# A recurrence in chunks: half of its level products on the off-diagonal quadrants of TensorE, and both parts of the output summed in PSUM

## What is computed

```
def step(s, inp):
    r_t, w_t, k_t, v_t, a_t, b_t = inp
    sa = jnp.einsum('bhvk,bhk->bhv', s, a_t)
    s = s * w_t[:, :, None, :] + sa[..., :, None] * b_t[:, :, None, :] + v_t[..., :, None] * k_t[:, :, None, :]
    return s, jnp.einsum('bhvk,bhk->bhv', s, r_t)
```

## Time and profile before

| | us |
|---|---|
| median of 3 runs (lowest, highest) | 2602.45 (2600.98, 2603.02) |
| the profiled execution, its own time | 2604.29 |
| its span in the trace | 2602.5 |
| TensorE busy in the span | 2314.5 (89%) |
| VectorE busy | 1688.6 (65%) |
| ScalarE busy | 1025.3 (39%) |
| GpSimd busy | 661.3 (25%) |
| granted TensorE clock, mean over the span | 0.933 |

### The profile page before, as it was taken

The page is one execution under the profiler, slowest core; times in us unless marked ns, Lnnn a source line. Parts: engine busy times, 40 slices in busy tenths (PEclk is TensorE's granted clock), DMA queues, the critical chain, the costliest instruction groups (busy, mean ns, idle before and its releaser), DMA issues. The chain is left out here.

```text
span 2602.5 us, 50127 instructions
## 1 busy us (share of the span) xinstructions
PE 2314.5 (89%) x20892; PEld 1847.3 (71%) x20892; DVE 1688.6 (65%) x2155; ACT 1025.3 (39%) x1633; POOL 661.3 (25%) x659
## 2 busy tenths in 40 slices
PE   5998988899999669999777999999973999999993
PEld 2886755568877558888636899997652888888883
DVE  5990559551115445666576776774657999999994
ACT  3112541231014420001154545444132877777773
POOL 1331568123320023222006666650000100000000
PEclk8998999999999779999878999998986999999997
DMA  6232004421104445211053111104142999999994
GB/s 237 96 124 75 1 33 142 132 99 45 49 14 185 151 156 193 96 41 40 14 185 92 32 32 29 29 20 169 57 174 97 409 407 396 396 393 405 396 378 158
DMA packets 136485, 401.77 MB, mean 154 GB/s; under 512 B 56314, under 2 KB 67834, under 8 KB 108754
## 3 DMA queue, kind: packets, MB, share of 16 engines
q1 hardware_dynamic: 124180, 360.02, 37.3%
q0 software_dynamic: 4608, 16.78, 2.7%
q10 hardware_dynamic: 7488, 21.99, 2.2%
HBM read 341.05 MB, written 57.69 MB: 153 GB/s over the span
## 5 line engine op out<-in xcount | busy, mean ns | idle before, releaser
L3900 DVE TENSOR_TENSOR ex_wl<-ew_raw,ex_wh 128x2048 fp32r<-128x2048 f32 x192 | 435.6, 2290 | 41.7 <-ACT ex_wh L3862 38.2
L3862 ACT ACTIVATE ex_wh<-ew_raw 128x2048 fp32r<-128x2048 f32 x192 | 367.6, 1919 | 109.5 <-PE ex_U L3806 40.3
L118 PE MATMUL sp_acc<-b2h_hi,sp_wh 128*128 128x512 f32 (+1 forms) x528 | 194.7, 369 | 16.2 <-POOL sp_wl L1729 16.2
L118 PE MATMUL sp_acc<-b2h_lo,sp_wh 128*128 128x512 f32 (+1 forms) x528 | 194.4, 368 | 0.0
L118 PE MATMUL sp_acc<-b2h_hi,sp_wl 128*128 128x512 f32 (+1 forms) x528 | 194.2, 368 | 0.0
L3783 POOL DMA_INDIRECT x<-ex_o,ex_at x16 | 26.5, 1656 | 490.2 <-DVE ex_o L3923 490.2
L2621 PE MATMUL rc_chain<-rc_x,rc_near 64*64 64x64 f32 x3200 | 132.8, 222 | 5.3 <-DVE rc_near L2503 2.2
L1727 POOL CAST sp_wh<-sp_w 128x1024 fp32r<-128x1024 f32 x26 | 28.3, 1088 | 402.2 <-DMA sp_w<-in_w_conv 221.4
L2621 PEld LDWEIGHTS rc_chain<-rc_x,rc_near 64*64 64x64 f32 x3200 | 111.1, 135 | 19.2 <-issue 9.0
L118 PEld LDWEIGHTS sp_acc<-b2h_hi,sp_wh 128*128 128x128 f32 x528 | 100.1, 190 | 33.9 <-POOL sp_wl L1729 16.6
L118 PEld LDWEIGHTS sp_acc<-b2h_lo,sp_wh 128*128 128x128 f32 x528 | 100.2, 190 | 16.4
(11 more groups left out here) (520 smaller groups left out, 5887.6 us busy)
## 6 DMA issues: line engine op xcount, KB each, us to landing
ew_raw<-in_exp_gate SPq DMA_DIRECT2D x64, 1024.0 KB, 8.0
ew_raw<-in_exp_up SPq DMA_DIRECT2D x64, 1024.0 KB, 9.5
ew_raw<-in_exp_down SPq DMA_DIRECT2D x64, 1024.0 KB, 8.0
b2p_pT<-in_ada_w SPq DMA_DIRECT2D x32, 512.0 KB, 6.0
...
```

Source lines behind the costliest of these rows:

```text
L118: ins = nc.tensor.matmul(out, w[a][:, k, :], h[b][:, k, cols], start=(first and n == 0), stop=(last and n == 2))
L3862: nc.scalar.activation(wh[:, n % RING], raw[:, n % RING], ACT.Copy).then_inc(q["w_hi"], 1)
L3900: V.tensor_tensor(wl[:, n % RING], raw[:, n % RING], wh[:, n % RING].bitcast(f32), ALU.subtract).then_inc(q["w_lo"], 1)
```

## The change

`chained_x` and `advanced` send half of their eight products (heads 2 and 3 of the four tiles, j = 1) through the off-diagonal quadrants. For that x is kept with its two row halves swapped in those tiles after the first product and swapped back after the second. The transposes must then swap the halves too: one `turned` becomes three instructions, one 128x128 in place and two of 64x128 that write the other half. Both products now go to PSUM as two banks of 128 columns. `outputs_of_state` is gone on TensorE and VectorE; its products accumulate in the same PSUM region as those of `outputs`, in four groups of four 64x64 and four 128x64 products. The hand-written orders of four engines are new; of GpSimd's and ScalarE's the diff below leaves the lists out, and of the other two the removed lines.

```diff
@@ -2132,7 +2132,7 @@
-        joint = {n: ph.sem(n) for n in ("firsts_done", "xi_done", "g_crossed", "g_done", "u_done", "y_done", "y_crossed", "s_done", "rows_done", "v_done")}
+        joint = {n: ph.sem(n) for n in ("firsts_done", "xi_done", "g_crossed", "g_done", "u_done", "y_crossed", "s_done", "rows_done", "v_done")}
...
@@ -2157,9 +2157,9 @@
-        def chained(d, bank):
-            return X[d][:, bank, 0:HP * CK].rearrange("p (h t) -> p h t", t=CK)
+        def chained(d):
+            return X[d][:, :, 0:2 * CK].rearrange("p j (f t) -> p j f t", t=CK)
@@ -2293,7 +2293,7 @@
                         if c >= 2:
                             pool.wait_ge(s["low_done"], c - 1)
                         if c >= CTX_CK + 2:
-                            pool.wait_ge(joint["y_done"], c - 1 - CTX_CK)
+                            pool.wait_ge(joint["y_crossed"], c - 1 - CTX_CK)
                         G.tensor_tensor(b["ar"][:, c % 2, :, CK:], rows(RB, c, d), b["e_in"], ALU.mult).then_inc(s["r_scaled"], 1)
@@ -2323,26 +2323,26 @@
...
@@ -2380,14 +2380,14 @@
                 def filled(c, d):
                     if runs(c):
                         if c >= 2:
-                            act.wait_ge(q[d]["xt_next"], LEVELS * (c - 1))
+                            act.wait_ge(q[d]["xt_next"], 3 * LEVELS * (c - 1))
                             act.wait_ge(q[d]["t1_done"], LEVELS * (c - 1))
                         A.activation(t[d]["x"][:, c % 2], spread(T.ident2[:], 1, HP), ACT.Copy, scale=-1.0).then_inc(q[d]["filled"], 1)
                 def factored(c, d, l):
                     if runs(c):
                         act.wait_ge(q[d]["t1_done"], LEVELS * c + l + 1)
-                        A.activation(t[d]["t1"][:], chained(d, 0), ACT.Copy).then_inc(q[d]["t1_ready"], 1)
+                        A.activation(paired(t[d]["t1"][:]), chained(d), ACT.Copy).then_inc(q[d]["t1_ready"], 1)
                     if runs(c):
...
@@ -2506,7 +2506,7 @@
                     if runs(c):
                         b, s = t[d], q[d]
                         dve.wait_ge(s["xp_done"], (LEVELS - 1) * c + l + 1)
-                        V.copy_predicated(b["x"][:, c % 2], spread(T.level[d][l + 1][:].bitcast(u32), 1, HP), chained(d, 1)).then_inc(s["x_next"], 1)
+                        V.copy_predicated(paired(b["x"][:, c % 2]), over(T.level[d][l + 1][:].bitcast(u32)), chained(d)).then_inc(s["x_next"], 1)
                 def turned(c, d, l):
                     if runs(c):
@@ -2517,7 +2517,14 @@
                                 dve.wait_ge(joint["xi_done"], c)
                         else:
                             dve.wait_ge(s["x_next"], (LEVELS - 1) * c + l)
-                        V.transpose(b["xt"][:].rearrange("p h t -> p (h t)"), b["x"][:, c % 2].rearrange("p h t -> p (h t)")).then_inc(s["xt_next"], 1)
+                        def flat(m):
+                            return m.rearrange("p h t -> p (h t)")
+                        near_half, far_half = slice(0, 2), slice(2, 4)
+                        V.transpose(flat(b["xt"][:, near_half]), flat(b["x"][:, c % 2, near_half])).then_inc(s["xt_next"], 1)
+                        for p in range(2):
+                            src, to = slice(p * CK, (p + 1) * CK), slice((1 - p) * CK, (2 - p) * CK)
+                            V.transpose(flat(b["xt"][to, far_half]), flat(b["x"][src, c % 2, far_half])).then_inc(s["xt_next"], 1)
                 def last_factor(c, d):
                     if runs(c):
@@ -2525,7 +2532,7 @@
                         dve.wait_ge(s["t1_done"], LEVELS * c + LEVELS)
                         if c:
                             dve.wait_ge(joint["xi_done"], c)
-                        V.copy_predicated(b["last_t"][:], spread(T.level[d][LEVELS][:].bitcast(u32), 1, HP), chained(d, 0)).then_inc(s["t1_ready"], 1)
+                        V.copy_predicated(paired(b["last_t"][:]), over(T.level[d][LEVELS][:].bitcast(u32)), chained(d)).then_inc(s["t1_ready"], 1)
                 def right_side(c, d):
                     if runs(c):
@@ -2534,21 +2541,12 @@
                         dve.wait_ge(s["g_copied"], c + 1)
                         V.tensor_tensor(b["g"][:], part(V_, d), b["g"][:], ALU.add).then_inc(s["g_ready"], 1)
-                def outputs_of_state(c, d):
-                    if runs(c, CTX_CK):
-                        n = c - CTX_CK
-                        dve.wait_ge(joint["y_done"], n + 1)
-                        for o in range(2):
-                            dve.wait_ge(q[o]["y_added"], 2 * n + 1)
-                        yv = y[:, :, y_at(c, d):y_at(c, d) + CK]
-                        V.tensor_tensor(yv, part(V_, d), yv, ALU.add).then_inc(q[d]["y_added"], 1)
                 def outputs(c, d):
                     if runs(c, CTX_CK):
                         n = c - CTX_CK
                         dve.wait_ge(joint["y_crossed"], n + 1)
                         for o in range(2):
-                            dve.wait_ge(q[o]["y_added"], 2 * n + 2)
+                            dve.wait_ge(q[o]["y_added"], n + 1)
                         yv = y[:, :, y_at(c, d):y_at(c, d) + CK]
                         V.tensor_tensor(paired(yv), crossed(d), paired(yv), ALU.add).then_inc(q[d]["y_added"], 1)
@@ -2569,39 +2567,37 @@
                 for d in range(2):
                     dve.sem_inc(q[d]["state"], 1)
                     dve.sem_inc(q[d]["y_added"], 1)
-                for k in range(NCK + 1):
+                for k in range(NCK + 2):
+                    outputs(k - 2, 1)
+                    advanced(k - 1, 0, 1)
+                    advanced(k - 1, 1, 1)
+                    outputs(k - 2, 0)
+                    turned(k - 1, 0, 2)
+                    turned(k - 1, 1, 2)
+                    summed(k - 2, 1)
+                    summed(k - 2, 0)
+                    advanced(k - 1, 0, 2)
+                    advanced(k - 1, 1, 2)
+                    turned(k - 1, 0, 3)
+                    turned(k - 1, 1, 3)
+                    first(k, 1)
+                    advanced(k - 1, 0, 3)
                     first(k, 0)
...
+                    turned(k - 1, 0, 4)
                     advanced(k - 1, 1, 3)
                     last_factor(k - 1, 0)
...
                     turned(k - 1, 1, 4)
                     last_factor(k - 1, 1)
                     masked(k, 0)
+                    right_side(k - 1, 1)
                     right_side(k - 1, 0)
                     masked(k, 1)
                     turned(k, 0, 0)
...
                     turned(k, 1, 0)
                     advanced(k, 0, 0)
                     advanced(k, 1, 0)
                     turned(k, 0, 1)
...
                     turned(k, 1, 1)
...
                     if 4 <= k < 8:
                         weigh(dve, k - 4)
@@ -2614,11 +2610,17 @@
                     for j, s, c in product(range(HP // 2), range(2), range(2)):
                         yield j, c ^ s ^ d, c
-                def diagonal(d, bank, l, r):
-                    for h, p in product(range(HP), range(2)):
-                        k = slice(p * CK, (p + 1) * CK)
-                        last = M(chained(d, bank)[k, h], l(h, p)[k], r[k, h], start=True, stop=True)
+                def quarters():
+                    for f, j, p in product(range(2), range(HP // 2), range(2)):
+                        yield 2 * j + f, j, f, p, p ^ j
+                def chain(d, back, l, r):
+                    for h, j, f, p, o in quarters():
+                        frm, to = (o, p) if back else (p, o)
+                        k = slice(frm * CK, (frm + 1) * CK)
+                        last = M(chained(d)[to * CK:(to + 1) * CK, j, f], l(h, p)[k], r[k, h], start=True, stop=True)
                     return last
                 def crossing(l, r):
@@ -2685,19 +2687,19 @@
                             pe.wait_ge(s["x_ready"], c + 1)
                         else:
                             pe.wait_ge(s["x_next"], (LEVELS - 1) * c + l)
-                        diagonal(d, 0, lambda h, p: b["near"][:, c % 2, h % 2, 0, h - h % 2 + p], b["x"][:, c % 2]).then_inc(s["t1_done"], 1)
+                        chain(d, False, lambda h, p: b["near"][:, c % 2, h % 2, 0, h - h % 2 + p], b["x"][:, c % 2]).then_inc(s["t1_done"], 1)
                 def advanced(c, d, l):
                     if runs(c):
                         b, s = t[d], q[d]
                         pe.wait_ge(s["t1_ready"], LEVELS * c + l + 1)
-                        pe.wait_ge(s["xt_next"], LEVELS * c + l + 1)
-                        diagonal(d, 1, lambda h, p: b["xt"][:, h], b["t1"]).then_inc(s["xp_done"], 1)
+                        pe.wait_ge(s["xt_next"], 3 * (LEVELS * c + l + 1))
+                        chain(d, True, lambda h, p: b["xt"][:, h], b["t1"]).then_inc(s["xp_done"], 1)
                 def inverted(c):
                     if runs(c):
                         each("t1_ready", LEVELS * c + LEVELS)
```

(37 more changed lines are left out.)

118 lines of the change are left out of this document (43 added, 75 removed).

## The result

The changed kernel takes 2647.7 us, median of four runs (2637.4 to 2648.9), the kernel before beside it 2601.7: a ratio of 1.0169, 95% interval [1.0142, 1.0195]. **Slower, as forecast, but by 46 us instead of 16**, and outside the range of 2580 to 2640. The profiled execution took 2647.35, its span is 2645.6.

A forecast was written before the change was run, and what follows sets the result against it. TensorE's list bounds the kernel before, VectorE's the changed one. 15 full chunks x 0.93 = +14.0, context chunks +0.4, last `outputs` block +1.8: together +16, 2619 beside the median 2602.45; range 2580 to 2640.

The forecast's parts named there:

- Mechanism: Full chunks: the bound moves from TensorE to VectorE, whose slots become 18.1 us against TensorE's 16.0.
- The walk: Step by step through one full chunk at slot prices: a period of 20.7 us, +0.93 against 19.77.
- the slot of a held start: VectorE's transposes that cross partitions: 0.33 us from start to start, so three take 0.98 for a `turned`.
- the step "18.1 against 17.99": Context chunks, without outputs: VectorE goes on at 1.6 instead of 3.8, period 18.1 us against 17.99; +0.4 for three.
- rival 4: Granted clock falls to 1.2 GHz in stretches as TensorE pauses 4.7 us a chunk: 2640 and more; chance 0.05.
- Head and tail: Ends of the recurrence: no term for the first chunk; the last chunk's `outputs` block adds 1.8 us.
- Rival 1: VectorE's crossing transposes are not held back: `turned` 0.62, chunks 18.5, kernel 2579; chance 0.21, the errata formula's 0.03 included.
- turning point: Price of a start across partitions on VectorE: at about 0.28 us instead of 0.33 the kernel is even.
- Rival 2: TensorE's shape changes inside `outputs` cost nothing: 0.9 a chunk less, chunks 19.8, kernel 2604; chance 0.09.
- Rival 3: TensorE's level products do not run four abreast: slots 20.2, period some 22.4, kernel 2645; chance 0.05.
- The rule of the Trainium skill: VectorE instruction starting in another 32-partition quadrant waits until all earlier ones finish; gives the same 0.98 for a `turned`.
- TRN2 errata formula: VectorE takes 58 cycles and one per element: 128-wide transpose 0.19 us, `turned` about 0.67, kernel some 2584; chance 0.03.

The follow-up runs named there:

- e1: Changed kernel with the two crossing transposes replaced by two in-place 128x128 ones, the second into a scratch tile (computes with other data): 2599.4 us.
- e2: Changed kernel with level products in place and far transposes by row half without crossing, lower half first: 2640.1 us.
- e4: Changed kernel with both directions' transposes interleaved by place for levels 0 to 3, so that neighbours share their start: 2626.1 us.
- e18: The changed kernel itself run once more, nothing altered: 2642.1 us.
- e6: Changed kernel with `outputs` issuing its 16 state products first and its 16 stacked ones behind them, two shape changes instead of eight: 2620.3 us.
- e5: Changed kernel with its order and summed outputs, but level products in place and a single 128x256 transpose for a `turned`: 2624.5 us.

## Why the forecast was right in direction and wrong in size

- **Mechanism: right, its size too small.** VectorE's list became the bound; without the held starts nothing is left of the loss (e1, with e2 and e4 on what holds them). The walk met the trace from `outputs`(1) (3.43 forecast, 3.40 measured) to advanced(0,2) (7.5, 7.51), and drifted from there: last_factor(1) 13.7 against 13.89, masked(1) 16.3 against 16.62, the turned of level 0 17.5 against 17.83, the chunk 20.7 against 21.2. The mis-sized term is the period of a full chunk. Of its 0.5 about 0.24 is the slot of a held start, 0.337 for 0.327 (a third of 0.98) over the 24 on the way; the rest came at the hand-overs behind last_factor(1), and no run takes it apart. 15 x 0.5 = 7.5 us.
- **Context chunks: the step "18.1 against 17.99" failed.** At full clock they take 19.02 (e18). VectorE's busy 17.4 us leave it hardly a wait, but the walk let it go on 2.2 us sooner and took all of that off the chunk. 3 x 0.9 = 2.8 us.
- **Clock: the step that set it apart as rival 4, at 0.05, failed; by the estimate below it was the largest term missed.** It came true beside the forecast, as a further cost of the case held likeliest. Three falls in context chunks cost 4.0 us, those in two full chunks 2.6. The first full chunk has two more (0.85) and takes 21.91; in e2 and e4, at full clock, it is 1.5 to 2.0 shorter than the next, so an estimate from these puts its falls at 2.2 to 2.7 (the forecast took it for as long as the others). That is about 9 of the 29 us that were missed, with parts of the first chunk and of the last stretch on top. That TensorE's waits (2.6 us a chunk: 18.57 busy of 21.19) bring the falls on was the forecast's reason; e1, with 2.0 and no fall, leaves it unproven.
- **Head and tail: costed at nothing and at 1.8.** The last stretch, from the last `lower`(·, 0), is 31.2 instead of 25.2, +6.1; its `outputs` groups are 0.62 apart at the low clock, instead of 0.38:

```profile
1818.62 0.51 PEld L2735 LDWEIGHTS rc_crossing<-rc_ar,rc_S 64*64 64x64 f32 x8
1819.24 0.51 PEld L2738 LDWEIGHTS rc_crossing<-rc_near,rc_uv 128*64 128x64 f32 x8
```

  In e6, without a fall there and with a block shorter by 0.9, the stretch takes 27.9, so some 2.4 of the 6.1 are the clock. The first chunk is +3.1, and its start 1.6 sooner.
- The 25.0 of the full chunks are 14.0 as forecast, 7.5, 2.6, and 0.7 by which the first one is over 21.2; 0.2 is left. In sum 25.0 + 7.2 (context) + 3.1 + 6.1 - 1.6 = 39.8 of the recurrence, and 3.6 of another stage.
- **Rival 1 (transposes not held)** fell: they are held, 1.01 for three. e1 tests what it would have given: even then 19.8 a chunk, not 18.5. So the turning point "about 0.28 instead of 0.33" was wrong as well: the kernel is even at 0.19 to 0.23. **Rival 2** (shape changes free) fell: 0.15 each, twice (e5's block, e6). **Rival 3** fell: 32 loads in 0.56.
- The rule of the Trainium skill that was weighed ("VectorE: DVE Perf Modes", "Two Vector instructions with no wait between them") holds in all of e1, e2 and e4: next starts 0.19 apart where nothing moves, 0.33 to 0.34 where a start moves. The same page's TRN2 errata formula, 0.19 us for a 128-wide transpose, does not: the trace has 0.27 to 0.31. The same section says itself that this row comes out too low for single instructions and that the fixed term measured is about 150 cycles, by which it would be 0.29, an estimate that the trace bears out.
